# A seventh quad in seven-product form in each MLP block, with its weight sums made on GpSimd

## What is computed

```python
def squared_relu_mlp(h, w_up, w_down):
    a = jnp.square(jax.nn.relu(h @ w_up))
    return a @ w_down

def reference(x, ...):
    for layer in range(DEPTH):                      # DEPTH = 2
        h = rmsnorm(x, ln_mix_g[layer])
        x = x + (sb_fox_mixer if layer % 2 == 0 else mla_mixer)(h, ...)
        h = rmsnorm(x, ln_mlp_g[layer])
        x = x + squared_relu_mlp(h, mlp_w_up[layer], mlp_w_down[layer])
    return x
```

## Time and profile before

| | |
|---|---|
| median of 3 runs | 2055.92 us (2055.69 to 2056.04) |
| the profiled execution, its own time | 2056.3 us |
| its span, first to last instruction | 2054.6 us |
| granted TensorE clock | 1.000 of full speed |
| TensorE (PE) busy | 2044.1 us, 99% |
| VectorE (DVE) busy | 1503.0 us, 73% |
| ScalarE (ACT) busy | 1127.3 us, 55% |
| GpSimd (POOL) busy | 239.7 us, 12% |
| DMA queue of SyncE / of GpSimd | 55.3% / 12.6% of the 16 DMA engines' span |

### The profile page before, as it was taken

How to read it: one execution, slowest core, us unless ns; L and a number is a source line. 1 busy time by engine, 2 the same in 40 slices (tenths; PEclk the granted TensorE clock), 3 DMA queues, 4 the chain that set the end, 5 groups by cost and what they waited for, 6 DMA issues and landing times.

```text
span 2054.6 us, 26622 instructions
## 1 busy us (share of the span) xinstructions
PE 2044.1 (99%) x10464; PEld 1750.7 (85%) x10464; DVE 1503.0 (73%) x2063; ACT 1127.3 (55%) x1620; POOL 239.7 (12%) x349
## 2 busy tenths in 40 slices
PE   9999999999999999999999999999999999999999
PEld 7898888888888888888889888788888888888887
DVE  6556558867966877786696788877786696687777
ACT  5555565654644544554466786564554464454454
POOL 0000002020210120110010255101110021012010
PEclk9999999999999999999999999999999999999999
DMA  8555557685885795697576434768696588679565
GB/s 282 176 154 181 174 165 225 205 255 197 259 265 193 234 289 177 200 305 208 188 245 188 157 123 142 220 220 247 199 304 201 196 259 264 199 229 288 180 199 190
DMA packets 225780, 440.75 MB, mean 215 GB/s; under 512 B 12588, under 2 KB 27000, under 8 KB 225656
## 3 DMA queue, kind: packets, MB, share of 16 engines
q1 hardware_dynamic: 200520, 380.29, 55.3%
q0 software_dynamic: 25088, 58.73, 12.6%
q10 hardware_dynamic: 48, 0.02, 0.0%
HBM read 436.91 MB, written 2.10 MB: 214 GB/s over the span
## 4 chain that ended last, share of the span: by engine, by line
PE 95%; DVE 2%; ACT 1%; issue 1%; DMA 0%; SPq 0%; ACTq 0%; DVEq 0%
PE psum L1773 23%; PE psum L1726 13%; PE psum L1728 13%; PE psum L1727 13%; PE psum L1776 12%; PE psum L2060 6%; PE psum L2062 6%; PE psum L2061 6%; PE psum L1855 1%; DVE halves L1216 1%; PE psum L1942 1%; ACT halves L889 1%; PE psum L1797 1%; PE psum L1919 0%; PE psum L1943 0%
## 5 line engine op out<-in xcount | busy, mean ns | idle before, releaser
L1216 DVE TENSOR_TENSOR halves<-raw,halves 128x1024 fp32r<-128x1024 f32 (+2 forms) x736 | 847.4, 1160 | 393.1 <-ACT halves L889 389.1
L889 ACT CAST halves<-raw 128x1024 fp32r<-128x1024 f32 (+2 forms) x736 | 724.0, 996 | 551.4 <-PE psum L1728 247.9
L1773 PE MATMUL psum<-h,halves 128*128 128x512 f32 x2048 | 490.0, 391 | 0.0
L1773 PEld LDWEIGHTS psum<-h,halves 128*128 128x128 f32 x2048 | 376.2, 188 | 72.7
L1726 PE MATMUL psum<-halves,a 128*128 128x512 f32 x700 | 275.4, 393 | 0.3 <-ACT mix L956 0.3
L1728 PE MATMUL psum<-halves,a 128*128 128x512 f32 x700 | 272.8, 390 | 0.0
L1727 PE MATMUL psum<-halves,a 128*128 128x512 f32 x700 | 272.4, 389 | 0.0
L1776 PEld LDWEIGHTS psum<-h,halves 128*128 128x128 f32 x2048 | 262.7, 191 | 10.0
L1776 PE MATMUL psum<-h,halves 128*128 128x256 f32 x2048 | 266.1, 283 | 0.0
L1726 PE MATMUL psum<-halves,h 128*128 128x512 f32 (+4 forms) x572 | 213.4, 373 | 1.1 <-DVE h L1287 1.0
L1728 PE MATMUL psum<-halves,h 128*128 128x512 f32 (+4 forms) x572 | 206.9, 362 | 0.0
(11 more groups left out here) (286 smaller groups left out, 2296.6 us busy)
## 6 DMA issues: line engine op xcount, KB each, us to landing
raw<-in_mlp_w_up SPq DMA_DIRECT2D x128, 1024.0 KB, 6.2
raw<-in_mlp_w_down SPq DMA_DIRECT2D x128, 1024.0 KB, 5.2
mix<-in_mlp_w_down POOLq DMA_DIRECT2D x192, 256.0 KB, 7.0
raw<-in_sf_w_in SPq DMA_DIRECT2D x41, 1024.0 KB, 5.1
raw<-in_sf_w_o SPq DMA_DIRECT2D x16, 1024.0 KB, 5.3
raw<-in_mla_w_o SPq DMA_DIRECT2D x16, 1024.0 KB, 5.1
raw<-in_mla_w_ukv SPq DMA_DIRECT2D x8, 1024.0 KB, 5.6
raw<-in_sf_w_in SPq DMA_DIRECT2D x14, 512.0 KB, 4.0
```

What stands on the lines that cost most here:

```text
L889: nc.scalar.copy(half_piece(n, 0), raw_piece(n)).then_inc(hi_done, 1)
L1216: v.tensor_tensor(half_piece(n, 1), raw_piece(n), half_piece(n, 0).bitcast(F32), ALU.subtract)\
L1773: last = mm(bank, half_piece(n, 0)[:, cols], src[:, k].rearrange("p s t -> p (s t)"), start=(k == 0), stop=(k == KT - 1))
```

## The change

In each MLP block quad 5 becomes a fast quad, so seven of eight are, with only quad 2 plain. VectorE no longer makes the MLPs' weight sums: `weight_sums` moves to GpSimd's queue, as two tensor-tensor additions of 128 x 512 for each fast quad, between the DMAs that GpSimd issues. SyncE's `free_slot` also waits for the sums that read a slot. Where both quads of a load of column 2 are fast, only the rows that `b22` needs are loaded (half a load). The seventh quad's token sums get a buffer in `sd_nat`, and the token sums are placed anew in the up stage.

```diff
-FAST_QUADS = 0, 1, 3, 4, 6, 7
-PLAIN_QUADS = 2, 5
+FAST_QUADS = 0, 1, 3, 4, 5, 6, 7
+PLAIN_QUADS = 2,
-U_BUFFER = 0, 1, 2, 3, 0, 1
+U_BUFFER = 0, 1, 2, 3, 0, 1, 2
...
                 if load >= SLOTS:
                     sp_.wait_ge(lo_done, LAST_OF[load - SLOTS] + 1 + extra)
+                    if load - SLOTS in SUMS_OF:
+                        sp_.wait_ge(t_step, SUMS_OF[load - SLOTS])
...
                 def down(load, c, l):
-                    fetch(load, w_down[b0 * D + 4 * P * l:b0 * D + 4 * P * (l + 1), c * N:(c + 1) * N])
+
+                    both_fast = c == 2 and 2 * l in FAST_QUADS and 2 * l + 1 in FAST_QUADS
+                    fetch(load, w_down[b0 * D + 4 * P * l:b0 * D + 4 * P * (l + 1), c * N:(c + 1) * N], both_fast)
...
+            def weight_sums(layer, b0, m):
+
+                base, no, q = block_base(layer, b0), block_no(layer, b0), FAST_QUADS[m]
+                one, _ = pair_loads(layer, b0, q // 2)
+                at, u, t = q % 2 * 2 * N, u_sum[U_BUFFER[m]], v_sum[m % 2]
+                b11, b21 = (raw[:, one % SLOTS, at + k * N:at + (k + 1) * N] for k in range(2))
+                pool.wait_ge(lo_done, base + (32 if m < 2 else quad_at(FAST_QUADS[m - 2]) + 3))
+                pool.wait_ge(raw_loaded[one % SLOTS], 16 * (one // SLOTS + 1))
+                pool.wait_ge(u_summed[m % 2], summed_count(no, m))
+                pool.tensor_tensor(t[:, 0], b11, u[:, 1], ALU.add).then_inc(t_step, 1)
+                pool.wait_ge(t_step, stepped_count(no, m) - 1)
+                pool.tensor_tensor(t[:, 1], b21, t[:, 0], ALU.add).then_inc(t_step, 1)
+
             def neighbour_sums(layer):
                 for b0 in range(NB):
-                    for m in (0, 2, 4):
+                    for m in (0, 1):
                         u_load(layer, b0, m)
-                        u_load(layer, b0, m + 1)
+                    for m in (0, 1):
                         u_add(layer, b0, m)
-                        u_add(layer, b0, m + 1)
+                    for m in (2, 3):
+                        u_load(layer, b0, m)
+                    for m in (2, 3):
+                        u_add(layer, b0, m)
+                    weight_sums(layer, b0, 0)
+                    weight_sums(layer, b0, 1)
+                    u_load(layer, b0, 4)
+                    u_load(layer, b0, 5)
+                    weight_sums(layer, b0, 2)
+                    u_add(layer, b0, 4)
+                    u_add(layer, b0, 5)
+                    weight_sums(layer, b0, 3)
+                    u_load(layer, b0, 6)
+                    weight_sums(layer, b0, 4)
+                    u_add(layer, b0, 6)
+                    weight_sums(layer, b0, 5)
+                    weight_sums(layer, b0, 6)
...
-                        if c == 1 and j == 3:
-                            token_sums_hi(no, 1)
+                        if c in (1, 3) and j == 3:
+                            token_sums_hi(no, (1, 4)[c // 2])
...
-                    for at, slot, bank in ((quad_at(7) - 1, 3, X8), (quad_at(7), 0, X1)):
+                    for at, slot, bank, m in ((quad_at(7) - 1, 3, X8, 3), (quad_at(7), 0, X1, 6)):
                         if j == at:
                             act.wait_ge(pieces_used, base + at + 1)
-                            act.wait_ge(lo_done, base + quad_at(FAST_QUADS[3]) + 2)
+                            act.wait_ge(lo_done, base + quad_at(FAST_QUADS[m]) + 2)
...
-            def weight_sums(layer, b0, m):
-
-                q = FAST_QUADS[m]
-                one, _ = pair_loads(layer, b0, q // 2)
-                half_sums(one, q % 2, u_sum[U_BUFFER[m]], block_no(layer, b0), m)
-
...
-                        if c == 1 and j == 2:
-                            token_sums(no, 1)
-                        if c == 1 and j == 4:
-                            token_sums_lo(no, 1)
+                        if c in (1, 3) and j == 2:
+                            token_sums(no, (1, 4)[c // 2])
+                        if c in (1, 3) and j == 4:
+                            token_sums_lo(no, (1, 4)[c // 2])
...
-                    if j in sums:
-                        weight_sums(layer, b0, sums[j])
```

More of the change, by code:

```diff
@@ L161, in summed_count @@
 def summed_count(no, m):
-    return 32 * (fast_before(no) // 2 + m // 2 + 1)
+    of_kind = [len((OUT_FAST if i % (NB + 1) == 0 else FAST_QUADS)[m % 2::2]) for i in range(no)]
+    return 32 * (sum(of_kind) + m // 2 + 1)
 def stepped_count(no, m):
@@ L212, in all_pieces, with sums_of_loads @@
     return out
+def sums_of_loads():
+    out = {}
+    for layer in range(2):
+        for b0 in range(NB):
+            for m, q in enumerate(FAST_QUADS):
+                out[pair_loads(layer, b0, q // 2)[0]] = stepped_count(block_no(layer, b0), m)
+    return out
 PIECES = all_pieces()
+SUMS_OF = sums_of_loads()
 LAST_OF = {PIECES[n][1]: n for n in sorted(PIECES) if PIECES[n][0] in ("raw", "b22")}
@@ L417, in build @@
         halves = sb("halves", [P, SLOTS, 2, 2 * N], F32R)
-        with nc.sbuf_tensor("sd_nat", [P, 4, 2, P], F32R) as sd_nat:
+        with nc.sbuf_tensor("sd_nat", [P, 2, 4, 2, P], F32R) as sd_nat:
             pass
@@ L503, in sd_of @@
         def sd_of(i):
-            return sd[:, i] if i < 4 else (sd_last, sd_nat)[i - 4][:]
+            return sd[:, i] if i < 4 else sd_last[:] if i == 4 else sd_nat[:, i - 5]
         def out_sd(i):
@@ L655, in mlp_block, with fetch @@
                 load0 = block_load(layer, b0)
-                def fetch(load, src):
+                def fetch(load, src, second_rows=False):
                     free_slot(load)
-                    sp_.dma_start(raw[:, load % SLOTS].rearrange("p (k n) -> p k n", k=4),
-                                  src.rearrange("(k p) n -> p k n", p=P)).then_inc(raw_loaded[load % SLOTS], 16)
+                    dst, src = raw[:, load % SLOTS].rearrange("p (q k n) -> p q k n", q=2, k=2), \
+                        src.rearrange("(q k p) n -> p q k n", q=2, p=P)
+                    if second_rows:
+                        dst, src = dst[:, :, 1], src[:, :, 1]
+                    else:
+                        dst, src = dst.rearrange("p q k n -> p (q k) n"), src.rearrange("p q k n -> p (q k) n")
+                    sp_.dma_start(dst, src).then_inc(raw_loaded[load % SLOTS], 16)
                 def down(load, c, l):
-                    fetch(load, w_down[b0 * D + 4 * P * l:b0 * D + 4 * P * (l + 1), c * N:(c + 1) * N])
+                    both_fast = c == 2 and 2 * l in FAST_QUADS and 2 * l + 1 in FAST_QUADS
+                    fetch(load, w_down[b0 * D + 4 * P * l:b0 * D + 4 * P * (l + 1), c * N:(c + 1) * N], both_fast)
                 for c in range(4):
@@ L1176, in mlp_block @@
                     nc.scalar.copy(a[:, 4 * c:4 * c + 4, 0, :], y_buf).then_inc(y_hi, 1)
-                    token_sums_hi(no, c + 1 if c else 0)
+                    token_sums_hi(no, (0, 2, 3, 5)[c])
                 for j in range(32, BLOCK_PIECES):
@@ L1181, in mlp_block @@
                     if j == 34:
-                        token_sums_hi(no, 5)
-                    for at, slot, bank in ((quad_at(7) - 1, 3, X8), (quad_at(7), 0, X1)):
+                        token_sums_hi(no, 6)
+                    for at, slot, bank, m in ((quad_at(7) - 1, 3, X8, 3), (quad_at(7), 0, X1, 6)):
                         if j == at:
                             act.wait_ge(pieces_used, base + at + 1)
-                            act.wait_ge(lo_done, base + quad_at(FAST_QUADS[3]) + 2)
+                            act.wait_ge(lo_done, base + quad_at(FAST_QUADS[m]) + 2)
                             nc.scalar.copy(c_sum[:, slot], bank).then_inc(joint_copied, 1)
@@ L1646, in mlp_block @@
                         if c and j == 1:
-                            token_sums_lo(no, c if c > 1 else 0)
-                        if c == 1 and j == 2:
-                            token_sums(no, 1)
-                        if c == 1 and j == 4:
-                            token_sums_lo(no, 1)
+                            token_sums_lo(no, (0, 2, 3)[c - 1])
+                        if c in (1, 3) and j == 2:
+                            token_sums(no, (1, 4)[c // 2])
+                        if c in (1, 3) and j == 4:
+                            token_sums_lo(no, (1, 4)[c // 2])
                         if b0 == 0 and c == 0 and j == 2:
@@ L1665, in mlp_block @@
                                     ALU.subtract).then_inc(split_done, 1)
-                    token_sums(no, c + 1 if c else 0)
-                sums = {34: 0, 37: 1, quad_at(2) - 3: 2, quad_at(3) - 1: 3, quad_at(5) - 2: 4, quad_at(6) - 1: 5}
+                    token_sums(no, (0, 2, 3, 5)[c])
                 end = quad_at(8)
@@ L1687, in mlp_block @@
                     if j == 33:
-                        token_sums_lo(no, 4)
-                        token_sums(no, 5)
+                        token_sums_lo(no, 5)
+                        token_sums(no, 6)
                     if j == 35:
```

(4 more changed lines are left out.)

## The result

The changed kernel takes **2141.08 us**, the median of 4 runs (2140.04 to 2142.13), against 2055.92 before: a ratio of 1.0414, 95% interval 1.0402 to 1.0426. Slower was forecast, but by 24 us; it is 85, and outside the range of 2053 to 2110. The profiled execution took 2141.15 us, with a span of 2139.3.

What follows compares the result with a forecast made beforehand. TensorE, busy for 99% of the span, was taken as the bound. Eight blocks, each 3.72 us late less 0.68 for fewer matmuls, add 24.3 to 2056.3: 2080.6, forecast as 2080 us; range 2053 to 2110.

Steps and rivals of the forecast that it cites:

- The mechanism: In the MLP sets, GpSimd's additions and VectorE's splits take turns at SBUF, 1.1 us per addition; forecast case, 0.55.
- The rivals in which they run side by side, wholly or in part: In the sets, additions delay no split, 2050.5 (0.14), or part of them falls in gaps, 2053 to 2065 (0.14).
- the queue as the bound: GpSimd's queue in the set: a sum behind an `u_add` waiting for loads comes late, 2096 and more; chance 0.17.
- column 0: VectorE in column 0 loses two sums (2.6), is held up for four additions (4.4), 18.5 + 1.8 of 21.9: nothing.
- The set: VectorE splits quad 7's raw piece at 37.7 us, TensorE wants it at 34.0: 3.7 us late per block.
- What was to be shown: Changed profile: 24 matmuls fewer, splits over 2 us, additions 1.1 to 2.3, some 30 us of TensorE waits, sets of 42.
- the forecast's own walk: VectorE's order in the set from 7.18 us: plain pieces 1.14, fast quads 4.03, additions 1.1 each.
- DMA, SyncE's wait, ScalarE, token sums at nothing: Loads, SyncE's slot wait, ScalarE's 1.5 more pieces and up's extra token sums were each priced at nothing.
- the first rival: In the sets, GpSimd's additions run beside VectorE's splits and delay none: 2050.5 us; chance 0.14.
- The seventh quad's gain of 5.4 us: On TensorE, quad 5 loses 3 matmuls, eight times: 24 x 0.2267 = 5.44 us, 0.68 a block.

Runs made afterwards that it cites:

- the unread sums: Changed kernel with t24 in the MLPs cut from the content of t13, so no split waits for GpSimd's sums: 2130.22 us.
- the fills: Changed kernel with each of GpSimd's two additions replaced by a zero fill of the whole sum buffer, sums left out: 2059.74 us.
- the best arrangement: Changed kernel, sums back on VectorE, earlier buffer and load for m = 6, sums of m = 3 and 4 made earlier: 2058.69 us, 1.0013.

## Why the prediction was right in its sign and wrong in its size

- **The mechanism held.** Additions and splits take turns: 1.09 us of VectorE per turn, where 1.1 was taken. The rivals in which they run side by side, wholly or in part, are out by the splits of 2.31 us; the queue as the bound is out by the unread sums, which save 11 us of 85.
- **The step that failed is column 0,** "VectorE loses two sums (2.6) and is held up for four additions (4.4), 18.5 + 1.8 of 21.9: nothing". It cost 37.3 us, 44% of the loss. The 4.4 was right (4.07 measured on the chain). Wrong was to set it against the stage's mean: the additions were let go by piece 32, and from 2.2 us into the stage all four fell on the one chain there that has about 1 us to spare. A walk piece by piece, as was made for the set, would have given 4.4 - 1 = 3.4 us of stop a block, 27 in all, where 25.3 was measured; the 11.9 us of slower matmuls behind the stops no row of before could price.
- **The set was mis-sized,** 3.7 us late by the forecast, 6.7 measured (45.5 in this block against the bare 38.77). Two parts are named by rows. The forecast looked only at quad 7's raw piece; by its own sum quad 6's t13 is the later one: 7.18 + 2 x 1.14 + 3 x 4.03 + 2 x 1.14 + 11.0 = 34.8, wanted after 4.76 x 5 + 5.44 + 6 x 0.2267 = 30.6, so 4.2 late. And VectorE gives up 12 turns, not 10, as two additions sit behind DMAs (11 in the last two blocks): 2.2 more, 6.4. In the trace that piece's split is done at 556.01, and TensorE's last stop of the set ends there:

```profile
553.70 2.31 DVE L1266 TENSOR_TENSOR halves<-mix,halves 128x1024 fp32r<-128x1024 f32 x1
```

```profile
556.06 0.50 PE L2101 MATMUL psum<-halves,sd_nat 128*128 128x512 f32 x1 [0.51 <-DVE halves L1266]
```

- **What was to be shown:** 24 matmuls fewer, as forecast. Splits over 2 us and additions of 1.3 to 2.3, as forecast, but the two of 3.50 and 1.98 take two turns each. Waits in the MLPs' sets 36.9 us instead of some 30, and sets of 45.3 instead of 42. The stops are at quads 2, 4, 5 and 6, not at 5 to 7. The one at quad 2 the forecast's own walk has too: 7.18 + 2 x 1.1 + 1.14 = 10.5, wanted at 2 x 4.76 = 9.5, so 1.0 late; measured 1.14.
- **DMA, SyncE's wait, ScalarE, token sums at nothing:** the fills bound them together. With everything of the change but the additions' reads the time is 2059.74, some 9 us over the 2050.5 of the first rival, at the landings and sums that ScalarE waits for; in the changed kernel such waits are near none (0.6 us for accumulating DMAs, 0.6 for sums). There ScalarE waits 26.1 us for loads instead, all in column 3, where TensorE doesn't stop. The token sums' moves cost nothing seen: up keeps its length.
- **The seventh quad's gain of 5.4 us** was reached by no order tried, not even with VectorE's sums. Over a whole set VectorE has the time: 7 x 4.03 + 2.28 + 5 x 1.32 = 37.1 us against 38.77 of matmuls. But a fast quad with its sum takes it 4.03 + 1.32 = 5.35 us against TensorE's 4.76, and in the best arrangement, 39.76 a set where the kernel before has 39.44, TensorE stops twice, at the first pieces of quads 6 and 7, which VectorE splits right behind their sums. Whether another order would gain is open.

## What to carry to other kernels

When work is moved to an engine whose instructions take turns with another's, walk the receiving stage piece by piece: a stage with 15% of free time may open with a chain that has next to none, and the time at which the moved work is let go decides between nothing and a stop. Price such work in the other engine's turns, and count the turns, not the instructions. Before work is moved off the nearly full engine, ask whether one more unit of it can be followed at all: here a fast quad with its sum is 5.35 us of VectorE against 4.76 of TensorE, and no order tried made up for it.

## What the runs showed of the hardware

- An addition on GpSimd issued while that engine was still busy with four accumulating DMAs lasted 3.50 us and held up two of VectorE's splits by 1.2 and 1.1 us; with a fill between them it lasted 1.91 us and the split beside it was 0.13 longer.
- Of eight stops of TensorE of 2.83 to 3.19 us, six were followed by matmuls that started 0.43 us apart instead of 0.2267 (for some 3 us after the one shown); after two, of 2.83 and 3.13 us, the granted clock stayed at 1.00. In the sets, stops of up to 1.7 us left it at 1.00.
- A 128x512 addition on GpSimd takes 1.28 us at the least and mostly 1.7 to 2.2 beside the splits; a fill of 128x1024 takes mostly 0.96 and slows no split (1.23 us at the most).
